# Seven block products for eight in two row pairs of the first feed-forward weight product

## The chip, the cores and the metric

One core of one Trainium2 chip. The metric is the device time of one execution of the whole program in microseconds (us), the median of several runs.

## The reference, cut to what matters

Two transformer blocks over 256 tokens of width 2048, in float32. The change is in the first block's feed-forward part:

```
h   = rmsnorm(x, ffn_norm_g)                  # 256 x 2048
hid = h @ w_ffn_in                            # 2048 x 11264, the product that changes
x   = x + (silu(hid[:, :5632]) * hid[:, 5632:]) @ w_ffn_out
```

The other large products of the first block are `h @ w_in` before it and, after it, a gate; the second block has `h @ w_up` and `@ w_down` of the same sizes.

## The kernel before, in words

Activations lie in SBUF as tiles of 128 features x 256 tokens and are the matmuls' stationary side; weights stream through as the moving side. Every float32 factor is split into a rounded part ("hi") and a remainder ("lo"), and a product is three matmuls: hi x hi, hi x lo, lo x hi, each 128 x 128 by 128 x 512.

**Granules.** A weight matrix is cut into chunks of 512 output columns, and each chunk into granules of 256 input rows (a "row pair", p): 128 partitions x 1024 columns, 512 KB. w_ffn_in has 22 chunks of 8 granules; a chunk holds 256 gate columns and the 256 up columns that belong to them. For each granule SP starts a DMA into one of four slots of `raw` (L827); ACT casts it to `wh` (L894); DVE takes the remainder into `wl` (L1242); PE does 12 matmuls (L1785), two row tiles by two token halves by three. `wh` and `wl` too have four slots: the cast of granule i waits until PE has done granule i - 4, and the DMA of granule i waits for the remainder of granule i - 4.

**Order.** One list, `plan`, holds for every step the things to do; each engine walks the same list in order and takes what is its own, waiting on semaphores. Step s holds the cast and remainder of granule s, the fetch of granule s + 4, whatever `later` put there, and the matmuls of granule s - 3. Chunk results are drained from step (last granule + 4) on.

**Drain of this stage.** `plan_gated` (L473): `silu` on ACT (L1084, L1085) from the chunk's two PSUM banks into `ST`, the first half of the scratch tile `tmp`; `gated` on DVE (L1526, L1529) multiplies it. After every second chunk, one step later, a `turn` on DVE (L1336, L1338) transposes the 512 columns of two chunks into `Y`; POOL writes `Y` to DRAM (L1742) and, two steps after the turn, gathers it back transposed as `Z` (L1750); eight steps after that, `split_hi` (ACT, L1053, L1054) and `split_lo` (DVE, L1497, L1499) make the tiles `act1` of the next product. Chunks 0 and 1 are done side by side (six granules of each, then two of each); the others one after another, in two alternating pairs of PSUM banks.

**Units of seven.** Two products of the kernel, `out1` (act1 @ w_ffn_out) and `down`, already do some row pairs another way. `product_side_by_side` (L312) runs two chunks together, a granule of one and then of the other, and at row pairs listed in `SEVEN` treats the two granules as one 2 x 2 x 2 block product done with seven block products (21 matmuls) in place of eight (24). Such a unit needs: `base_hi` (ACT, L911), a 1536-wide cast into a buffer of its own; `sums` (DVE, L1269, L1272, L1274: 1024, 512 and 512 wide) into `tile_sums`, which is `tmp`; `base_lo` (DVE, L1255), 1536 wide; `forms_hi` (ACT, L917) and `forms_lo` (DVE, L1278), 2048 wide, into two slots of `wh` and `wl`. They stand in the list in this order, in the step of the unit's second granule. PE does `multiply_base` (9 matmuls, after `base_lo`) and `multiply_forms` (12, after `forms_lo`). The fetches that reuse the two raw slots wait for `base_lo`. Four block products of each unit add up in four PSUM banks that the pair of chunks shares; after the pair's last unit `shared_out` (ACT, L930) copies them to `tile_sums`, and DVE adds them up and onto the rows `X`. The activations' own sums and differences are made once per stage (`xs_sum`, `xs_hi`, `xs_lo`).

Of the kernel before, what the change touches and what calls it, by code (L numbers as in the profile page):

```python
# [8 lines left out]
P = 128  # L9
# [35 lines left out]
SEVEN = (8, 10, 12, 14, 16, 18)  # L45
# [50 lines left out]
def two_block_kernel(nc, t, out):  # L96
    with ExitStack() as ctx:
# [124 lines left out]
        base_lo = view("base_lo", [P, 3, 512], o_a + 6 * K, FR)  # L222
        tile_sums = tmp.rearrange("p (k c) -> p k c", k=4)
        xs_hi = view("xs_hi", [P, 6, 3, P], o_a + 12 * K, FR)
        xs_lo = view("xs_lo", [P, 6, 3, P], o_a + 21 * K, FR)
        xs_in = view("xs_in", [P, 2, 4, P], o_a)
        xs_out = view("xs_out", [P, 2, 4, P], o_a + 4 * K)
# [41 lines left out]
        seven_operand = {"out1": "act1", "down": "act2"}  # L269
        side_by_side = {"out1": [], "down": []}  # L270
# [41 lines left out]
        def product_side_by_side(src, stage, q, bank, order, tail, afters, late, cleared):  # L312

            operand = seven_operand[stage]
            pair = Pair(stage, q, [], 4 - bank)
            side_by_side[stage].append(pair)
# [4 lines left out]
            rows = list(order[:tail])  # L321
            for u, p in enumerate(rows):
                if p in SEVEN:
                    former = list(seven.values())[-1] if seven else None
                    unit = Seven(len(granules), p, pair, former, SEVEN.index(p))
# [4 lines left out]
            for k, name in enumerate(("shared_out", "shared_sums", "shared_first", "shared_last", "shared_second")):  # L330
# [137 lines left out]
        def plan_x_sums(stage, step, every):  # L468
            for j in range(3):
                for k, name in enumerate(("xs_sum", "xs_hi", "xs_lo")):  # L470
                    later(step + every * j + k, lambda name=name, j=j: do(name, stage, j))

        def plan_gated(n):  # L473
            def after(s, chunk):
                chunk.drained = [("silu", n), ("gated", n)]
                do("silu", n)
                do("gated", n)

                def leave():
                    rows_of["act1", n // 2] = turn(s + 1, ST, ("gated", n))  # L480
                if n % 2:
                    later(s + 1, leave)
                    plan_split(("act1", n // 2), s + 11, "act1", n // 2)
# [95 lines left out]
        for n in range(2, 22):  # L579
            last_ffn = product(t["w_ffn_in"], "N", "ffn", PAIRS16, ("gated", n), plan_gated(n), n)  # L580
        plan_x_sums("out1", len(granules) + 4, 3)
        out_from = len(granules)
        for q in range(2):
            cleared = ([], []) if q == 0 else ([("shared_out", "out1", 0)], [("shared_out", "out1", 0)])
            product_side_by_side(t["w_ffn_out"], "out1", q, (4, 0)[q], OUT_ORDERS[q], OUT_TAILS[q],
                                 [plan_out(2 * q), plan_out(2 * q + 1)], 0, cleared)
# [74 lines left out]
        for q in range(2):  # L661
            cleared = ([("pool_out", 1)], [("x_split", 1, 1)]) if q == 0 else ([("shared_out", "down", 0)],) * 2
            product_side_by_side(t["w_down"], "down", q, (4, 0)[q], DOWN_ORDERS[q], DOWN_TAILS[q],
                                 [plan_down(2 * q), plan_down(2 * q + 1)], (5, 0)[q], cleared)
# [70 lines left out]

        def product_of(*key):
            return through(named[key])
# [51 lines left out]
        def seven_tiles(x, j):  # L789

            k = 2 * SEVEN[2 * j]
# [81 lines left out]
        def scalar(e):  # L873
# [8 lines left out]
            for name, args in phases:  # L882
# [19 lines left out]
                elif name == "base_hi":  # L902
# [4 lines left out]
                    if unit.pair.q == 0 and unit is unit.pair.units[0]:  # L907
                        e.wait_ge(*at("xs_lo", unit.pair.stage, 2))
                    else:
                        e.wait_ge(multiplied, multiply_count["multiply_base", unit.former.i])  # L910
                    e.copy(base_hi.rearrange("p k c -> p (k c)"), two_slots(raw, i)[:, 512:2048]).then_inc(done[name], 1)  # L911
# [6 lines left out]
                elif name == "xs_hi":  # L918
                    stage, j = args
                    e.wait_ge(*at("xs_sum", stage, j))  # L920
                    e.copy(seven_tiles(operands[seven_operand[stage]][0], j)[:, :, 1], xs_out[:, :, 0])
                    e.copy(xs_hi[:, 2 * j:2 * j + 2], xs_out[:, :, 1:4]).then_inc(done[name], 1)
                elif name == "shared_out":
# [5 lines left out]
                    for k in range(4):  # L929
                        e.copy(tile_sums[:, k, :], ps[:, pair.shared + k, :]).then_inc(done[name], 1)  # L930
# [145 lines left out]
                elif name == "silu":  # L1076
# [6 lines left out]
                    e.wait_ge(*product_of("gated", n))  # L1083
# [129 lines left out]
        def vector(e):  # L1213
# [22 lines left out]
            for name, args in phases:  # L1236
# [15 lines left out]
                elif name == "base_lo":  # L1252
                    i, = args
                    e.wait_ge(*at("base_hi", i))
                    e.tensor_tensor(base_lo.rearrange("p k c -> p (k c)"), two_slots(raw, i)[:, 512:2048],  # L1255
                                    base_hi.rearrange("p k c -> p (k c)").bitcast(F32), ALU.subtract).then_inc(done[name], 1)
                elif name == "sums":
# [22 lines left out]
                elif name == "xs_sum":  # L1280
                    stage, j = args
                    hi, lo = (seven_tiles(x, j) for x in operands[seven_operand[stage]])
                    if j == 0:

                        e.wait_ge(*through(last_ffn if stage == "out1" else last_up))
                    else:
                        e.wait_ge(*at("xs_lo", stage, j - 1))
                    e.wait_ge(*tile_at(seven_operand[stage], 2 * SEVEN[2 * j + 1] + 1))
                    e.tensor_tensor(xs_in[:], hi.bitcast(F32), lo.bitcast(F32), ALU.add).then_inc(vector_step, 1)  # L1289
                    e.wait_ge(vector_step, next(step))  # L1290
                    e.tensor_tensor(xs_out[:, :, 0:2], xs_in[:, :, 1:2].broadcast_to([P, 2, 2, P]), xs_in[:, :, 0:4:3],  # L1291
                                    ALU.subtract).then_inc(vector_step, 1)
                    e.wait_ge(vector_step, next(step))
                    e.tensor_tensor(xs_out[:, :, 2], xs_in[:, :, 0], xs_out[:, :, 1], ALU.subtract).then_inc(vector_step, 1)
                    e.wait_ge(vector_step, next(step))
                    e.tensor_tensor(xs_out[:, :, 3], xs_in[:, :, 2], xs_out[:, :, 2], ALU.subtract).then_inc(done[name], 1)
                elif name == "xs_lo":
                    stage, j = args
                    e.wait_ge(*at("xs_hi", stage, j))
                    hi, lo = (seven_tiles(x, j)[:, :, 1] for x in operands[seven_operand[stage]])  # L1300
# [3 lines left out]
                elif name == "shared_sums":  # L1304

                    stage, q = args
                    p1, p5, p6, p7 = (tile_sums[:, k, :] for k in range(4))
# [3 lines left out]
                    e.tensor_tensor(p7, p7, p6, ALU.add).then_inc(done[name], 1)  # L1311
                elif name == "shared_first":
# [4 lines left out]
                    e.tensor_tensor(X[:, 1, n0], X[:, 1, n0], tile_sums[:, 3, :], ALU.subtract).then_inc(done[name], 1)  # L1317
                elif name == "shared_last":
                    stage, q = args
                    e.wait_ge(*at("shared_first", stage, q))  # L1320
                    e.tensor_tensor(tile_sums[:, 2:4, :], tile_sums[:, 2:4, :],
                                    tile_sums[:, 1:2, :].broadcast_to([P, 2, 512]), ALU.add).then_inc(done[name], 1)
                elif name == "shared_second":
                    stage, q = args
                    n1 = slice(1024 * q + 512, 1024 * q + 1024)
                    e.wait_ge(*at("shared_last", stage, q))
                    e.tensor_tensor(X[:, :, n1], X[:, :, n1], tile_sums[:, 2:4, :], ALU.add).then_inc(done[name], 1)

# [436 lines left out]
        def tensor(e):  # L1765
# [42 lines left out]
            for name, args in phases:  # L1808
# [44 lines left out]
                elif name == "multiply_base":  # L1853
# [4 lines left out]
                    b11, b22, b21 = ([x[:, n, :] for x in (base_hi, base_lo)] for n in range(3))  # L1858
                    operand = seven_operand[pair.stage]
                    a11, a12 = ([x[:, k + n, 0:P] for x in operands[operand]] for n in range(2))  # L1860
                    s4 = [x[:, place, 2] for x in (xs_hi, xs_lo)]
                    if opens:
                        for phase in {("out1", 0): named["gated", 20].drained + named["gated", 21].drained,
                                      ("out1", 1): named["out1", 0].drained + named["out1", 1].drained,
                                      ("down", 0): named["up", 20].drained + named["up", 21].drained,
                                      ("down", 1): named["down", 0].drained + named["down", 1].drained}[pair.stage, pair.q]:
# [7 lines left out]
                elif name == "multiply_forms":  # L1874
# [5 lines left out]
                    s1, s2 = ([x[:, place, n] for x in (xs_hi, xs_lo)] for n in range(2))  # L1880
                    s3, a22 = ([x[:, k + n, P:T] for x in operands[seven_operand[pair.stage]]] for n in range(2))
# [129 lines left out]
def sevens(v):  # L2011
# [3 lines left out]
    for p in SEVEN:  # L2015
        first, second = v[:, 0, p].copy(), v[:, 1, p].copy()
        v[:, 0, p, :, 0], v[:, 0, p, :, 1] = second[:, :, 0], first[:, :, 0]
        v[:, 1, p, :, 0], v[:, 1, p, :, 1] = second[:, :, 1], first[:, :, 1]
# [73 lines left out]
```

## Time and profile before

| what | value |
|---|---|
| median of 3 runs | 2418.22 us (2418.18 to 2418.65) |
| the profiled execution | 2418.17 us, its span 2416.4 us |
| granted TensorE clock | 0.999 |
| PE busy | 2405.6 us (100%), 10666 matmuls |
| DVE busy | 1621.5 us (67%) |
| ACT busy | 1310.1 us (54%) |
| POOL busy | 189.4 us (8%) |
| DMA | 545.85 MB, mean 226 GB/s |

The page gives busy time by engine, the windows the same for a stretch, the timeline single instructions with start, length and, in brackets, how long the engine sat idle before and what released it. A matmul's length includes its way through the array, so that matmuls overlap. The longest idle times of the other engines are ACT's casts waiting for PE (883.7 us in 635 waits) and DVE's remainders waiting for the casts.

### The profile page before, as it was taken

What the parts mean: (1) busy time and instruction counts of PE and PEld (TensorE: products, weight loads), DVE (VectorE), ACT (ScalarE), POOL (GpSimd) and SP (SyncE); (2) the same over time, 40 slices, a digit from 0 to 9 for tenths busy, and PEclk for the clock granted to TensorE, in tenths of its full rate; (3) what the DMA queues carried; (4) which work ended last, traced back from release to release, by engine and by line L of the source; (5) the groups of instructions that cost most, each with busy time, mean ns of one, the idle gap of its engine ahead of it and who ended that gap; (6) DMA issues with size and microseconds to landing.
All of it is one profiled execution on the core that took longest, in us unless ns stands there. A gap on an engine that the chain in (4) does not pass through costs nothing.

```text
span 2416.4 us, 27837 instructions
## 1 busy us (share of the span) xinstructions
PE 2405.6 (100%) x10666; PEld 1993.9 (83%) x10666; DVE 1621.5 (67%) x2009; ACT 1310.1 (54%) x1608; POOL 189.4 (8%) x349
## 2 busy tenths in 40 slices
PE   9999999999999999999999999999999999999998
PEld 8888888888888888888888888888888888888887
DVE  7575555667555555569786865786567766678886
ACT  7555566445444444445455754545566666665554
POOL 0000000001000000000001110110111111110000
PEclk9999999999999999999999999999999999999999
DMA  8777665778777777676678777887788888886664
GB/s 278 224 223 226 200 192 178 221 233 253 221 211 226 215 212 225 210 217 210 198 230 272 243 237 216 254 249 234 238 245 245 241 244 240 240 248 209 215 204 160
DMA packets 155013, 545.85 MB, mean 226 GB/s; under 512 B 20096, under 2 KB 20608, under 8 KB 154624
## 3 DMA queue, kind: packets, MB, share of 16 engines
q1 hardware_dynamic: 131120, 470.91, 62.4%
q0 software_dynamic: 23184, 72.37, 11.2%
q8 instruction: 84, 1.38, 0.2%
q10 hardware_dynamic: 576, 0.79, 0.1%
q14 instruction: 49, 0.40, 0.1%
HBM read 505.72 MB, written 38.27 MB: 225 GB/s over the span
## 4 chain that ended last, share of the span: by engine, by line
PE 97%; DVE 2%; DMA 1%; ACT 0%; issue 0%; SPq 0%; DVEq 0%; ACTq 0%
PE ps L1785 96%; DVE wl L1242 0%; DMA raw<-in_w_down 0%; ACT wh L894 0%; PE ps L1924 0%; DMA XG<-in_x 0%; DVE xs_in L1289 0%; PE ps L1944 0%; DVE tmp L1666 0%; DVE xs_lo L1302 0%; DVE tmp L1269 0%; DVE tmp L1673 0%; DVE wl L1278 0%; DVE xs_out L1291 0%; ACT wh L917 0%
## 5 line engine op out<-in xcount | busy, mean ns | idle before, releaser
L1242 DVE TENSOR_TENSOR wl<-raw,wh 128x1024 fp32r<-128x1024 f32 x826 | 1007.1, 1222 | 749.5 <-ACT wh L894 748.5
L894 ACT CAST wh<-raw 128x1024 fp32r<-128x1024 f32 x826 | 863.8, 1049 | 897.1 <-PE ps L1785 883.7
L1785 PE MATMUL ps<-wh,x1g_hi 128*128 128x512 f32 x704 | 273.9, 389 | 0.0
L1785 PE MATMUL ps<-wl,x1g_hi 128*128 128x512 f32 x704 | 273.9, 389 | 0.0
L1785 PE MATMUL ps<-wh,x1g_lo 128*128 128x512 f32 x704 | 273.9, 389 | 0.0
L1785 PE MATMUL ps<-wh,x4g_hi 128*128 128x512 f32 x704 | 273.9, 389 | 0.0
L1785 PE MATMUL ps<-wl,x4g_hi 128*128 128x512 f32 x704 | 273.9, 389 | 0.0
L1785 PE MATMUL ps<-wh,x4g_lo 128*128 128x512 f32 x704 | 273.9, 389 | 0.0
L1785 PE MATMUL ps<-wh,h_hi 128*128 128x512 f32 x576 | 225.1, 393 | 0.8 <-ACT wh L899 0.8
L1785 PE MATMUL ps<-wh,h_lo 128*128 128x512 f32 x576 | 223.5, 390 | 0.0
L1785 PE MATMUL ps<-wl,h_hi 128*128 128x512 f32 x576 | 223.2, 390 | 0.0
L1785 PE MATMUL ps<-wh,act_hi 128*128 128x512 f32 x560 | 217.9, 389 | 0.0
L1785 PE MATMUL ps<-wl,act_hi 128*128 128x512 f32 x560 | 217.9, 389 | 0.0
L1785 PE MATMUL ps<-wh,act_lo 128*128 128x512 f32 x560 | 217.8, 389 | 0.0
L1750 POOL DMA_DIRECT2D Z<-rows x268 | 146.1, 552 | 363.9 <-DMA rows<-Y 351.7
L1742 POOL DMA_DIRECT2D rows<-Y x67 | 37.5, 560 | 1620.3 <-DVE Y L1338 1620.3
L1785 PEld LDWEIGHTS ps<-wl,x1g_hi 128*128 128x128 f32 x704 | 132.2, 188 | 27.6
L1785 PEld LDWEIGHTS ps<-wh,x4g_lo 128*128 128x128 f32 x704 | 132.1, 188 | 27.6
L1785 PEld LDWEIGHTS ps<-wh,x1g_hi 128*128 128x128 f32 x704 | 132.2, 188 | 27.3
L1785 PEld LDWEIGHTS ps<-wh,x1g_lo 128*128 128x128 f32 x704 | 132.2, 188 | 27.3
L1785 PEld LDWEIGHTS ps<-wh,x4g_hi 128*128 128x128 f32 x704 | 132.1, 188 | 27.4
L1785 PEld LDWEIGHTS ps<-wl,x4g_hi 128*128 128x128 f32 x704 | 132.1, 188 | 27.4
(348 smaller groups left out, 3560.6 us busy)
## 6 DMA issues: line engine op xcount, KB each, us to landing
raw<-in_w_in SPq DMA_DIRECT2D x196, 512.0 KB, 4.4
raw<-in_w_ffn_in SPq DMA_DIRECT2D x176, 512.0 KB, 3.7
raw<-in_w_up SPq DMA_DIRECT2D x176, 512.0 KB, 4.6
raw<-in_w_ffn_out SPq DMA_DIRECT2D x88, 512.0 KB, 4.3
raw<-in_w_down SPq DMA_DIRECT2D x88, 512.0 KB, 4.3
rows<-Y POOLq DMA_DIRECT2D x67, 512.0 KB, 5.6
Z<-rows POOLq DMA_DIRECT2D x268, 128.0 KB, 4.9
raw<-in_w_o SPq DMA_DIRECT2D x32, 512.0 KB, 4.7
```

What stands on the lines that cost most here:

```text
L894: e.copy(wh[:, i % RING, :], raw[:, slot, :]).then_inc(rounded, 1)
L1242: e.tensor_tensor(wl[:, r, :], raw[:, i % RAW, :], wh[:, r, :].bitcast(F32), ALU.subtract).then_inc(remainder, 1)
L1742: e.dma_start(rows_out[n % 2], Y[:]).then_inc(rows_left[n % 2], 16)
L1750: e.dma_start(ZA[32 * q:32 * q + 32], rows_out[n % 2, :, 256 * q:256 * q + 256].rearrange("(a i) e -> i a e", a=4)).then_inc(rows_back[n % ...
L1785: return e.matmul(dst, weights, x, start=start, stop=stop, skip_group_check=True)
```

## The change

In the first feed-forward product, eight pairs of chunks (2,3 to 16,17) run side by side. Of their eight row pairs, 4 and 6 are units of seven, in the order 0, 1, 4, 2, 6, 3, 5 and then row pair 7 of one chunk and of the other: so granules 4,5 and 8,9 of 16 are the units, and the chunks' last granules are 14 and 15. Chunks 0 and 1 stay as they were; 18 to 21 follow one after another as before, in other banks.

The pair alternates between PSUM banks 0 to 3 and 4 to 7, with the shared products in the other four. These are copied to `tile_sums` (`shared_out`), put together (`shared_sums`, `shared_last`), and, when a chunk is complete, added onto its banks in PSUM (`shared_bank`, DVE) ahead of its `silu`, which now waits for it. The first unit of a pair waits, in `sums`, for the turn of the pair before, since both use `tmp`; and PE's first shared product waits until the pair before is drained. The weights of rows 4 and 6 are swapped between the two chunks on the host, as for the other stages. Buffers for this stage (`gated_hi`, `gated_lo`, `gated_xs_hi` and so on) lie in the upper part of `act1`. In `out1` and `down` the shared tiles are put in other places and `shared_last` is two 512-wide operations in place of one of 1024.

```diff
-SEVEN = (8, 10, 12, 14, 16, 18)
+SEVEN = {"gated": (4, 6), "out1": (8, 10, 12, 14, 16, 18), "down": (8, 10, 12, 14, 16, 18)}
+GATED_PAIRS = range(1, 9)
+GATED_ORDER = (0, 1, 4, 2, 6, 3, 5, 7)
...
         def plan_gated(n):
             def after(s, chunk):
                 chunk.drained = [("silu", n), ("gated", n)]
+                if n // 2 in GATED_PAIRS:
+                    do("shared_bank", n)
                 do("silu", n)
                 do("gated", n)
...
-        for n in range(2, 22):
-            last_ffn = product(t["w_ffn_in"], "N", "ffn", PAIRS16, ("gated", n), plan_gated(n), n)
+        plan_x_sums("gated", len(granules), 0)
+        for q in GATED_PAIRS:
+            cleared = [] if q == 1 else [("shared_out", "gated", q - 1)]
+            product_side_by_side(t["w_ffn_in"], "gated", q, (0, 4)[q % 2], GATED_ORDER, 7, [plan_gated(2 * q), plan_gated(2 * q + 1)],
+                                 0, (cleared, cleared), ("shared_out", "shared_sums", "shared_last"))
+        for n in range(18, 22):
+            last_ffn = product(t["w_ffn_in"], "N", "ffn", PAIRS16, ("gated", n), plan_gated(n), n, (4, 6, 0, 2)[n - 18])
+            last_ffn.cleared = [("shared_out", "gated", 8)] if n < 20 else named["gated", n - 4].drained
...
+        def gated_at(n):
+
+            return at("shared_bank", n) if n // 2 in GATED_PAIRS else product_of("gated", n)
...
-                    e.wait_ge(*product_of("gated", n))
+                    e.wait_ge(*gated_at(n))
                     e.activation(ST[:, 0, sl], banks(chunk)[0][:, 0:T], ACT.Silu, scale=RT[:, 0:1]).then_inc(done[name], 1)
...
-                        e.wait_ge(*{("out1", 0): at("turn", rows_of["act1", 10]), ("out1", 1): at("shared_second", "out1", 0),
-                                    ("down", 0): at("act2_lo", 21), ("down", 1): at("squares", "out", 1)}[
-                                        unit.pair.stage, unit.pair.q])
+                        stage, q = unit.pair.stage, unit.pair.q
+                        e.wait_ge(*(at("turn", rows_of["act1", q - 1]) if stage == "gated" else {
+                            ("out1", 0): at("turn", rows_of["act1", 10]), ("out1", 1): at("shared_second", "out1", 0),
+                            ("down", 0): at("act2_lo", 21), ("down", 1): at("squares", "out", 1)}[stage, q]))
...
+                elif name == "shared_last":
+                    stage, q = args
+                    _, second, first, p5 = (tile_sums[:, k, :] for k in range(4))
+                    e.wait_ge(*at("shared_sums", stage, q))
+                    e.tensor_tensor(first, first, p5, ALU.add).then_inc(vector_step, 1)
+                    e.wait_ge(vector_step, next(step))
+                    e.tensor_tensor(p5, p5, second, ALU.add).then_inc(done[name], 1)
...
+                elif name == "shared_bank":
+                    n, = args
+                    bank0, bank1 = banks(named["gated", n])
+                    e.wait_ge(*product_of("gated", n))
+                    if n % 2 == 0:
+                        e.wait_ge(*at("shared_sums", "gated", n // 2))
+                        e.tensor_tensor(bank0, bank0, tile_sums[:, 0, :], ALU.add)
+                        e.tensor_tensor(bank1, bank1, tile_sums[:, 1, :], ALU.subtract).then_inc(done[name], 1)
+                    else:
+                        b = named["gated", n].bank
+                        e.wait_ge(*at("shared_last", "gated", n // 2))
+                        e.tensor_tensor(ps[:, b:b + 2, :], ps[:, b:b + 2, :], tile_sums[:, 2:4, :], ALU.add).then_inc(done[name], 1)
```

## Rows read from the trace of the kernel before

**Rows 1.** The page, part 1: busy time, share of the span and instructions of each engine.

```profile
PE 2405.6 (100%) x10666; PEld 1993.9 (83%) x10666; DVE 1621.5 (67%) x2009; ACT 1310.1 (54%) x1608; POOL 189.4 (8%) x349
```

**Rows 2.** The instructions on one operand of the feed-forward stage.

```profile
L1785 PE MATMUL ps<-wh,x1g_hi x704: 389/389/389, 593.0 to 1071.0; 128*128 128x512 f32 x176
```

**Rows 3.** Windows: length, busy PE, PEld, DVE, ACT, POOL, clock, DMA share, GB/s.

```profile
635.00:678.60 43.60, 43.60 (x194) 36.13 (x193) 23.65 (x25) 19.75 (x23) 2.74 (x5) 1.00 0.72 217
1200.96:1211.15 10.19, 10.19 (x46) 8.45 (x45) 8.84 (x8) 5.48 (x5) 0.00 (x0) 1.00 0.68 217
2236.00:2246.00 10.00, 8.94 (x38) 6.78 (x37) 8.94 (x8) 5.45 (x5) 0.00 (x0) 1.00 0.59 204
```

**Rows 4.** Timeline of DVE and ACT, one unit among dense ones (1201 to 1208).

```profile
1200.96 1.22 DVE L1269 TENSOR_TENSOR tmp<-raw 128x1024 f32<-128x1024 f32 x1
...
1202.94 0.69 DVE L1274 TENSOR_TENSOR tmp<-tmp,raw 128x512 f32<-128x512 f32 x1
1203.55 1.75 DVE L1255 TENSOR_TENSOR base_lo<-raw,base_hi 128x1536 fp32r<-128x1536 f32 x1
1205.68 2.29 DVE L1278 TENSOR_TENSOR wl<-tmp,wh 128x2048 fp32r<-128x2048 f32 x1 [0.39 <-ACT wh L917]
...
1203.74 1.92 ACT L917 CAST wh<-tmp 128x2048 fp32r<-128x2048 f32 x1 [1.46 <-DVE tmp L1274]
```

**Rows 5.** Timeline of ACT and DVE around one drained chunk, feed-forward stage.

```profile
723.78 1.05 ACT L894 CAST wh<-raw 128x1024 fp32r<-128x1024 f32 x1 [1.67 <-PE ps L1785]
724.73 0.47 ACT L1084 ACTIVATE tmp<-ps,small 128x256 f32<-128x256 f32 x1
725.10 0.47 ACT L1085 ACTIVATE tmp<-ps,small 128x256 f32<-128x256 f32 x1
...
724.86 1.22 DVE L1242 TENSOR_TENSOR wl<-raw,wh 128x1024 fp32r<-128x1024 f32 x1 [1.50 <-ACT wh L894]
726.00 0.48 DVE L1526 SCALAR_TENSOR_TENSOR tmp<-ps,small,tmp 128x256 f32<-128x256 f32 x1
726.40 0.47 DVE L1529 SCALAR_TENSOR_TENSOR tmp<-ps,small,tmp 128x256 f32<-128x256 f32 x1
...
728.73 0.70 DVE L1336 STREAM_TRANSPOSE Y<-tmp 128x512 f32<-128x512 f32 x1
729.36 0.67 DVE L1338 STREAM_TRANSPOSE Y<-tmp 128x512 f32<-128x512 f32 x1
```

**Rows 6.** Timeline of PE where a granule begins, same stretch.

```profile
723.52 0.39 PE L1785 MATMUL ps<-wh,x1g_hi 128*128 128x512 f32 x1
```

**Rows 7.** Timeline of DVE and PE, a unit of down whose load came late.

```profile
2236.53 1.23 DVE L1269 TENSOR_TENSOR tmp<-raw 128x1024 f32<-128x1024 f32 x1 [2.58 <-DMA raw<-in_w_down]
...
2239.13 1.75 DVE L1255 TENSOR_TENSOR base_lo<-raw,base_hi 128x1536 fp32r<-128x1536 f32 x1
2241.26 2.29 DVE L1278 TENSOR_TENSOR wl<-tmp,wh 128x2048 fp32r<-128x2048 f32 x1 [0.38 <-ACT wh L917]
...
2241.03 0.47 PE L1785 MATMUL ps<-base_hi,act_hi 128*128 128x512 f32 x1 [0.80 <-DVE base_lo L1255]
...
2243.61 0.50 PE L1785 MATMUL ps<-wh,xs_hi 128*128 128x512 f32 x1 [0.26 <-DVE wl L1278]
```

**Rows 8.** Loads issued 2240 to 2242, nothing beside them.

```profile
DMA to landing us min/median/max: 3.6/4.1/4.5
```

**Rows 9.** Loads issued 736 to 742, beside the gather.

```profile
L827 SPq DMA_DIRECT2D raw<-in_w_ffn_in x2: 328/328/328, 737.0 to 739.7; - x2
...
DMA to landing us min/median/max: 6.4/6.9/7.5
```

**Rows 10.** Timeline of POOL: the gather of the turned rows.

```profile
736.20 2.18 POOL L1750 DMA_DIRECT2D Z<-rows  x4 [5.05 <-DMA rows<-Y]
```

**Rows 11.** Groups by form: 512-wide on DVE, from PSUM and from SBUF.

```profile
L1680 DVE TENSOR_TENSOR tmp<-tmp 128x512 f32<-128x512 f32 x22 | 15.1, 684 | 0.0
...
L1509 DVE TENSOR_TENSOR X<-ps,X 128x512 f32<-128x512 f32 x12 | 8.2, 684 | 0.0
```

More of the change, by code:

```diff
@@ L268, in two_block_kernel @@
         seven = {}
-        seven_operand = {"out1": "act1", "down": "act2"}
-        side_by_side = {"out1": [], "down": []}
+        seven_operand = {"gated": "ffn", "out1": "act1", "down": "act2"}
+        side_by_side = {"gated": {}, "out1": {}, "down": {}}
+        onto_rows = ("shared_out", "shared_sums", "shared_first", "shared_last", "shared_second")
         turns = []
@@ L310, in product_pair, with product_side_by_side @@
                         then[n]()
-        def product_side_by_side(src, stage, q, bank, order, tail, afters, late, cleared):
+        def product_side_by_side(src, stage, q, bank, order, tail, afters, late, cleared, ends):
             operand = seven_operand[stage]
             pair = Pair(stage, q, [], 4 - bank)
-            side_by_side[stage].append(pair)
+            side_by_side[stage][q] = pair
             for n in range(2):
@@ L320, in product_side_by_side @@
                 pair.chunks.append(chunk)
-            rows = list(order[:tail])
-            for u, p in enumerate(rows):
-                if p in SEVEN:
+            for u, p in enumerate(order[:tail]):
+                if p in SEVEN[stage]:
                     former = list(seven.values())[-1] if seven else None
-                    unit = Seven(len(granules), p, pair, former, SEVEN.index(p))
+                    unit = Seven(len(granules), p, pair, former, SEVEN[stage].index(p))
                     pair.units.append(unit)
@@ L329, in product_side_by_side @@
                     granules.append((pair.chunks[n], src[2 * q + n, p], operand, 2 * p, u == 0, False))
-            for k, name in enumerate(("shared_out", "shared_sums", "shared_first", "shared_last", "shared_second")):
+            for k, name in enumerate(ends):
                 later(pair.units[-1].i + 5 + k, lambda name=name: do(name, stage, q))
@@ L1254, in vector @@
                     e.wait_ge(*at("base_hi", i))
-                    e.tensor_tensor(base_lo.rearrange("p k c -> p (k c)"), two_slots(raw, i)[:, 512:2048],
-                                    base_hi.rearrange("p k c -> p (k c)").bitcast(F32), ALU.subtract).then_inc(done[name], 1)
+                    hi, lo = (all_three(x) for x in bases[seven[i].pair.stage])
+                    e.tensor_tensor(lo, two_slots(raw, i)[:, 512:2048], hi.bitcast(F32), ALU.subtract).then_inc(done[name], 1)
                 elif name == "sums":
@@ L1316, in vector @@
                     e.tensor_tensor(X[:, 0, n0], X[:, 0, n0], tile_sums[:, 0, :], ALU.add)
[L1317 to L1322, printed above, removed]
+                    e.tensor_tensor(X[:, 1, n0], X[:, 1, n0], tile_sums[:, 1, :], ALU.subtract).then_inc(done[name], 1)
                 elif name == "shared_second":
@@ L1857, in tensor @@
                     opens, ends_here = unit is pair.units[0], unit is pair.units[-1]
-                    b11, b22, b21 = ([x[:, n, :] for x in (base_hi, base_lo)] for n in range(3))
+                    b11, b22, b21 = ([x[:, n, :] for x in bases[pair.stage]] for n in range(3))
                     operand = seven_operand[pair.stage]
                     a11, a12 = ([x[:, k + n, 0:P] for x in operands[operand]] for n in range(2))
-                    s4 = [x[:, place, 2] for x in (xs_hi, xs_lo)]
+                    s4 = x_forms(unit)[3]
                     if opens:
[L1863 to L1866, printed above, removed]
+                        former = {"out1": ("gated", 20), "down": ("up", 20)}[pair.stage] if pair.q == 0 else (
+                            pair.stage, 2 * pair.q - 2)
+                        for phase in named[former].drained + named[former[0], former[1] + 1].drained:
                             e.wait_ge(*at(*phase))
@@ L2008, in stream, with sevens @@
     return np.ascontiguousarray(v).reshape(n // 512, k // 256, P, 1024)
-def sevens(v):
+def sevens(v, pairs, chunks):
     n, k, _, _ = v.shape
     v = v.reshape(n // 2, 2, k, P, 2, 512).copy()
[L2015 to L2018, printed above, removed]
+    for q in chunks:
+        for p in pairs:
+            first, second = v[q, 0, p].copy(), v[q, 1, p].copy()
+            v[q, 0, p, :, 0], v[q, 0, p, :, 1] = second[:, 0], first[:, 0]
+            v[q, 1, p, :, 0], v[q, 1, p, :, 1] = second[:, 1], first[:, 1]
     return np.ascontiguousarray(v.reshape(n, k, P, 1024))
```

83 lines of the change are left out of this document (54 added, 29 removed).

## The prediction

> **What bounds the kernel now.** I read the page first: PE is busy for 2405.6 of 2416.4 us [rows 1], so time goes only if matmuls go or PE starts to wait. A busy time of 0.389 us per matmul isn't its price, since matmuls overlap; the start-to-start step is. The first and last of 704 starts of the feed-forward stage [rows 2] are 478.0 us apart over 703 groups of three matmuls: 478.0 / 2109 = 0.2267 us. A granule (12 matmuls) costs PE 2.72 us, a pair of chunks (16) 43.5 us, a unit of seven block products (21 matmuls) 4.76 us. The windows show DVE busy 23.65 and ACT 19.75 of 43.6 us in today's stage [rows 3]: a wide cover on average. The question is the order in which these two queues work at the boundary of two pairs.
>
> **The gain.** Each unit has 21 matmuls for 24. Eight pairs with two units: 48 matmuls fewer, 48 x 0.2267 = 10.9 us. Nothing else leaves PE.
>
> **What is added to DVE and ACT.** Per unit, sums, base_lo and forms_lo take from the start of the sums to the end of forms_lo 1205.68 + 2.29 - 1200.96 = 7.01 us; the first third of it, until the cast of the forms starts on ACT, 2.78, and base_lo is done after 4.34 [rows 4]. The two plain remainders that this replaces cost 2 x 1.14 (start to next start) [rows 5]. Per pair also come four ACT copies and four 512-wide sums of the shared products, and the bank adds. DVE is then at some 38 of 42 us. shared_out, shared_sums, shared_last and split_lo come at granules 13 to 15, where the next chunks ask nothing of DVE, and where DVE has nearly half of its time free today [rows 3]; they cost nothing. Were that cover gone, the chain from point T below would start later by as much as DVE is late there. The one-off sums of the activations (1024 + 512 + 256 + 256 columns on DVE, a cast, a 1024-wide remainder: about 5 us at such prices) fall in pair 1's first granule, beside a ring of three filled granules, 8.2 us. POOL and SP get no new DMA; the loads behind a unit wait for base_lo instead of a remainder.
>
> **The boundary, step by step.** Name the granules of a pair 0 to 15 and those of the next 0' to 15'. The first chunk ends with 14, the second with 15. Now both are drained together, at the steps of 2' and 3', and the unit 4',5' follows at once; on DVE its sums stand behind the turn of these very chunks. Let B be the first matmul of granule 15. The cast of 2', which waits for 14, starts 0.26 us later: 723.52 against 723.78 [rows 5, 6]; call that T. PE then has 15, 0', 1', 2', 3' and wants the unit at B + 13.60 and its forms (nine matmuls on) at B + 15.64.
> - Cast 2' on ACT T to T + 1.05; remainder 2' on DVE from T + 1.08, next start T + 2.22 [rows 5].
> - shared_bank of the even chunk: two 512-wide adds, 0.60 apart (as 1202.94 and 1203.55 [rows 4]), done T + 3.50 with 0.68 for the second.
> - silu starts 0.11 after the add (DVE to ACT: 1202.94 + 0.69 to 1203.74 [rows 4]), T + 3.61, second half 0.37 later, done T + 4.45; today it follows its cast at once, 723.78 to 724.73 [rows 5]. **This wait holds ACT's queue**: the cast of 3', which could start at T + 2.72, stands behind it and starts at T + 4.35, done T + 5.40.
> - gated even fits in between. Remainder 3' T + 5.43, next start T + 6.57. shared_bank odd, 1024 wide, 1.22: T + 7.79. silu T + 7.90 to 8.74. gated odd starts T + 8.40, second half T + 8.80 to 9.27. Turn: two transposes, 0.63 and 0.67 [rows 5]: T + 9.30 to 10.60. Sums start at T + 10.63.
> - base_lo done T + 14.97 = B + 15.23. From such an end to the first matmul it takes 0.15 us (2239.13 + 1.75 to 2241.03 [rows 7]): B + 15.38 against 13.60, a wait of 1.8 us. forms_lo done T + 17.64, and 0.06 on (2241.26 + 2.29 to 2243.61 [rows 7]) the forms start at B + 17.96 instead of 15.64. **The first unit costs 2.32 us of waiting.**
> - The second unit, 8',9': its two loads go out after base_lo, at T + 15.0 and 15.4. A load takes 3.6 to 4.5 us where nothing is beside it [rows 8] and 6.4 to 7.5 beside the gather of the turned rows [rows 9]; the gather is issued some 6 us after the turn (729.36 + 0.67 to 736.20 [rows 5, 10]), here at T + 16.8, right upon them. DVE is free at T + 19.8. I take 6.0, between the two, since these loads start before the gather: landed T + 21.4, forms_lo 7.01 later, forms ready at B + 28.73. PE wants them at 17.96 + 2.72 + 5.44 + 2.04 = B + 28.16. Another 0.57; none at 4.5, and with 7.5 us 2.1.
>
> Seven boundaries (pairs 2 to 8) x 2.89 = 20.2 us. Pair 1 stands behind an old-style pair without shared_bank: its sums start some 5.7 us after the cast of 3', its forms are ready 0.1 late, its loads cost 0.5: 0.6 us. After pair 8 no unit follows, and the ring of four covers the late cast: nothing. out1 and down change by one 512-wide DVE op more per pair of chunks, beside plain tail granules: nothing. The drains that the shared banks wait for end at T + 9.3, before base_lo: nothing. **Sum: -10.9 + 20.2 + 0.6 = +9.9 us**, on the profiled execution's 2418.17 (the median of the runs, 2418.22, is the same): 2428.
>
> An operation with its output in PSUM on DVE has no row here. A read from PSUM costs nothing extra: L1509 684 ns, L1680 684 ns [rows 11]. I take the bank adds at these prices. From below nothing less is likely, as they are the fastest 512-wide rows; from above, 1.37 for the wide add if it ran as two: 0.15 per boundary, 1.1 us in all. The Trainium skill (VectorE: DVE Perf Modes, The TRN2 errata) says that a DVE operation pays 120 cycles of fixed cost from PSUM and 58 from SBUF, at 0.96 GHz some 0.065 us more, against the 684 and 684 ns above [rows 11]. By that rule three adds on the chain would add an estimated 0.19 us per boundary, 1.4 us in all.
>
> **Rivals.**
> 1. *The boundary wait is shorter than summed, and gain and loss cancel (same).* The 10.9 us are used up at 1.55 us per boundary. For it: unit 2's share of 0.57 hangs on one landing, and if the cast of 3' didn't stand behind the even silu, the chain would be 1.34 us shorter: 0.98 + about 0.55 per boundary, some 2418 in all. Against: both queues work in order, and every link above has a row. Chance 0.11.
> 2. *The cover holds (faster).* The sums of 4',5' start by T + 8.3, so that forms_lo ends under granule 3' and the base products, and the loads are back in time: then all 10.9 us stay, 2407. For it: today's DVE and ACT are idle for nearly half of the stage [rows 3], and the dense units at 1200 us run without any PE wait at DVE 8.84 of 10.19 us [rows 3]. Against: those have two plain remainders between units, not two drains and a turn; and where sums came late, at 2236.53 after a load, PE did wait, 0.80 us before the base products and 0.26 before the forms [rows 7]. It decides at 0.86 us per boundary. Chance 0.07.
> 3. *The loads cost more (slower still).* Both loads of the second unit take 7.5 us: 2.1 instead of 0.57 per pair, 8 x 1.5 = 12 more, 2440. For it, [rows 9]; against, these loads start before the gather and half of each should be done. Chance 0.12.
> 4. A wait of 2 us could cost clock besides. In the window with PE's wait of 0.80 the granted clock stays at 1.00 [rows 3]; I give it no time of its own.
>
> The forecast itself has 0.70. **Range:** the first unit's wait alone (7 x 2.32 - 10.9 + 0.1) gives 2423.7, with full load cost 2440; the cancelling case reaches down to 2418. I take 2419 to 2438, which leaves out rival 2, half of rival 1 and the top of rival 3. A measurement tells 0.2%, 4.8 us, from no change: faster 0.08, same 0.12, slower 0.80.
>
> **What would show it.** PE: 48 matmuls fewer; before the base products of the first unit of pairs 2 to 8 a gap of 1.8 us, released by base_lo, and some 0.5 more before their forms. ACT: 14 silus waiting for the bank adds, the next cast 1.6 us late. DVE: sums some 10.6 us after the cast of 2'. SP: loads held by base_lo. A pair at about 45.0 us instead of 43.5. It is wrong if PE idles less than 1 us at a boundary, if the bank adds take over 0.9 us for 512 columns, or if the second unit's base_hi doesn't wait for its load.

## The result, and the profile after

| | before | after |
|---|---|---|
| time, median of 4 runs each on the same chip | 2418.41 us (2418.18 to 2418.65) | 2443.14 us (2440.53 to 2444.89) |
| ratio, 95% interval | | 1.0101 (1.0088 to 1.0113) |
| profiled execution | 2418.17 us | 2444.39 us |
| its span | 2416.4 us | 2442.6 us |

The change costs 24.7 us where 9.9 were forecast, and the time lies above the range. The page, part 1 (busy time, share of the span, instructions of each engine), to be read against [rows 1]:

```profile
PE 2405.7 (98%) x10618; PEld 1983.8 (81%) x10618; DVE 1727.2 (71%) x2122; ACT 1341.4 (55%) x1641; POOL 189.4 (8%) x349
```

PE has its 48 matmuls fewer (10618 for 10666) but is no longer always busy: its share falls from 100% to 98%. The windows say where (length; busy PE, PEld, DVE, ACT, POOL; clock; DMA share; GB/s), first the whole stage and then one pair of chunks:

```profile
593.50:1096.90 503.40, 477.86 (x2064) 386.02 (x2063) 368.78 (x393) 248.91 (x286) 30.14 (x55) 1.00 0.67 208
651.16:697.68 46.52, 43.51 (x189) 34.73 (x188) 36.40 (x38) 23.11 (x26) 2.74 (x5) 1.00 0.65 205
```

The stage has grown from 478.6 to 503.4 us, by 24.8, and PE idles in 3.0 of a pair's 46.5 us, with DVE at 36.4. The 48 matmuls should have taken 10.9 away, so PE lost 35.7 us in this stage. (The profiled execution is 26.2 us longer in all; the other 1.4 lie outside the stage. 0.6 of them is one start of PE at 1638.5 that comes late by so much, and not in the traces of e1, e5 and e8.)

**The boundary of two pairs.** Timelines of ACT and then DVE (start, duration, engine, line, operation; in brackets the idle time before it and what ended it). They answer to [rows 5]; T, the cast of 2', is at 724.51:

```profile
724.51 1.05 ACT L926 CAST wh<-raw 128x1024 fp32r<-128x1024 f32 x1 [1.67 <-PE ps L1842]
728.14 0.48 ACT L1120 ACTIVATE tmp<-ps,small 128x256 f32<-128x256 f32 x1 [2.58 <-DVE ps L1380]
...
728.87 1.05 ACT L926 CAST wh<-raw 128x1024 fp32r<-128x1024 f32 x1
732.41 0.47 ACT L1120 ACTIVATE tmp<-ps,small 128x256 f32<-128x256 f32 x1 [2.50 <-DVE ps L1384]
```

```profile
726.73 0.69 DVE L1379 TENSOR_TENSOR ps<-ps,tmp 128x512 f32<-128x512 f32 x1
727.33 0.69 DVE L1380 TENSOR_TENSOR ps<-ps,tmp 128x512 f32<-128x512 f32 x1
...
731.09 1.23 DVE L1384 TENSOR_TENSOR ps<-ps,tmp 128x1024 f32<-128x1024 f32 x1
...
735.17 1.23 DVE L1306 TENSOR_TENSOR tmp<-raw 128x1024 f32<-128x1024 f32 x1
...
737.76 1.75 DVE L1292 TENSOR_TENSOR gated_lo<-raw,gated_hi 128x1536 fp32r<-128x1536 f32 x1
```

The first silu waits 2.58 us for the bank add, and the next cast stands behind it until T + 4.36. The sums of the unit 4',5' (L1306) start at T + 10.66, base_lo (L1292) ends at T + 15.00. What PE does with that, first for the unit 4',5' and then for 8',9' (timeline of PE):

```profile
739.66 0.47 PE L1842 MATMUL ps<-gated_hi,x1g_hi 128*128 128x512 f32 x1 [1.65 <-DVE gated_lo L1292]
...
742.23 0.50 PE L1842 MATMUL ps<-wh,gated_xs_hi 128*128 128x512 f32 x1 [0.25 <-DVE wl L1315]
...
751.77 0.47 PE L1842 MATMUL ps<-gated_hi,x1g_hi 128*128 128x512 f32 x1 [1.04 <-DVE gated_lo L1292]
...
754.35 0.50 PE L1842 MATMUL ps<-wh,gated_xs_hi 128*128 128x512 f32 x1 [0.25 <-DVE wl L1315]
```

Measured from the start of the matmul before, the one at 739.66 comes 1.80 us later than the usual step of 0.23 (1.65 of it idle), the one at 742.23 comes 0.42 later. The second unit is late too: 1.20 and 0.42. Its loads (the timeline of POOL, then the loads issued 738 to 742 with the least, median and longest time until they landed):

```profile
735.69 0.56 POOL L1799 DMA_DIRECT2D rows<-Y  x1 [40.47 <-DVE Y L1395]
739.19 2.18 POOL L1807 DMA_DIRECT2D Z<-rows  x4 [2.94 <-DMA rows<-Y]
```

```profile
L859 SPq DMA_DIRECT2D raw<-in_w_ffn_in x2: 327/380/432, 739.5 to 739.9; - x2
...
DMA to landing us min/median/max: 4.5/5.9/7.2
```

The later of the two loads took 7.2 us, and the gather (L1807) was issued at T + 14.7, a third of a microsecond ahead of the loads; in [rows 10] it came 5.6 us after the write of the rows, here 3.5. Over the stage the waits add up so (engine, line, what it waited for: us in total, times, longest):

```profile
ACT gated_hi L944 <- DMA raw<-in_w_ffn_in: 45.6, 8, 7.8
...
DVE tmp L1306 <- DMA raw<-in_w_ffn_in: 24.5, 8, 5.2
PE ps L1842 <- DVE gated_lo L1292: 21.7, 15, 3.4
...
ACT tmp L1120 <- DVE ps L1380: 20.7, 8, 2.6
```

PE waited 15 times for gated_lo: seven first units and eight second ones. Taking each late start against the step of 0.2267 us, with the matmul right behind each late one, which comes 0.08 or 0.11 us later than the step once more, the first units of pairs 2 to 8 lost 7 x 2.41 = 16.9 us, and the second units of pairs 1 to 8 lost 1.6, 1.4, 1.8, 1.8, 1.8, 2.4, 5.8 and 1.6, together 18.2. With 16.9 this is 35.1 of the 35.7.

### The profile page after: what moved, and what is told of

Read it like the earlier page. It is cut to its first block, busy times and chain, and to the rows that moved or that the text cites. A ratio compares the mean times of both kernels' runs of the same rounds, so it can differ in the third digit from the quotient of the medians.

```text
span 2442.6 us, 27959 instructions
## 1 busy us (share of the span) xinstructions
PE 2405.7 (98%) x10618; PEld 1983.8 (81%) x10618; DVE 1727.2 (71%) x2122; ACT 1341.4 (55%) x1641; POOL 189.4 (8%) x349
## 3 DMA queue, kind: packets, MB, share of 16 engines
q0 software_dynamic: 23184, 72.37, 10.9%
## 4 chain that ended last, share of the span: by engine, by line
PE 85%; DVE 7%; DMA 4%; ACT 2%; issue 2%; SPq 0%; POOL 0%; ACTq 0%; DVEq 0%; POOLq 0%
PE ps L1842 84%; DMA raw<-in_w_ffn_in 2%; DVE wl L1278 1%; DVE tmp L1306 1%; ACT wh L926 1%; DVE wl L1315 1%; ACT wh L950 1%; DVE gated_lo L1292 1%; DVE tmp L1309 1%; DVE tmp L1311 1%; DMA raw<-in_w_down 0%; DVE ps L1384 0%; DMA Z<-rows 0%; DVE Y L1395 0%; DMA rows<-Y 0%
## 5 line engine op out<-in xcount | busy, mean ns | idle before, releaser
L1278 DVE TENSOR_TENSOR wl<-raw,wh 128x1024 fp32r<-128x1024 f32 x794 | 964.5, 1222 | 630.7 <-ACT wh L926 629.3
L926 ACT CAST wh<-raw 128x1024 fp32r<-128x1024 f32 x794 | 828.2, 1049 | 767.1 <-PE ps L1842 751.6
L1842 PE MATMUL ps<-wh,x1g_hi 128*128 128x512 f32 x592 | 230.3, 389 | 0.0
L1842 PE MATMUL ps<-wl,x1g_hi 128*128 128x512 f32 x592 | 230.3, 389 | 0.0
L1842 PE MATMUL ps<-wh,x1g_lo 128*128 128x512 f32 x592 | 230.3, 389 | 0.0
L1807 POOL DMA_DIRECT2D Z<-rows x268 | 146.1, 552 | 354.1 <-DMA rows<-Y 341.6
L1842 PEld LDWEIGHTS ps<-wh,x1g_hi 128*128 128x128 f32 x592 | 111.1, 188 | 23.3
L1842 PEld LDWEIGHTS ps<-wl,x1g_hi 128*128 128x128 f32 x592 | 111.1, 188 | 23.1
L1842 PEld LDWEIGHTS ps<-wh,x1g_lo 128*128 128x128 f32 x592 | 111.1, 188 | 23.0
```

Source lines behind the costliest of these rows:

```text
L926: e.copy(wh[:, i % RING, :], raw[:, slot, :]).then_inc(rounded, 1)
L1278: e.tensor_tensor(wl[:, r, :], raw[:, i % RAW, :], wh[:, r, :].bitcast(F32), ALU.subtract).then_inc(remainder, 1)
L1807: e.dma_start(ZA[32 * q:32 * q + 32], rows_out[n % 2, :, 256 * q:256 * q + 256].rearrange("(a i) e -> i a e", a=4)).then_inc(rows_back[n % ...
L1842: return e.matmul(dst, weights, x, start=start, stop=stop, skip_group_check=True)
```

## The experiments

Four questions were open. Does the chain of in-order queues make the first unit late, and do its own loads, colliding with the gather, make the second unit late (my theory, which the expectations call A)? Or is all of it one lateness, which starts at the first unit and is handed on? Or has DVE too much work in this stage (36.4 of 46.5 us), so that any order gives such a time? And do PE's waits cost more than their length, by the clock? Eight kernels ran, each an edit of the changed kernel. The third column is the sum of PE's late starts in the stage of its trace, the fourth that sum less 10.9 us, the last the measured difference of the medians.

| kernel | us, median (lowest to highest, runs) | PE late, us | less 10.9 | measured |
|---|---|---|---|---|
| the change | 2443.14 (2440.53 to 2444.89, 4) | 35.1 | +24.2 | +24.7 |
| e1_gather | 2425.43 (2424.78 to 2425.93, 7) | 17.1 | +6.2 | +7.0 |
| e2_silus | 2432.26 (2431.65 to 2432.96, 4) | 23.8 | +12.9 | +13.8 |
| e3_order | 2417.45 (2417.00 to 2418.39, 10) | 9.6 | -1.3 | -1.0 |
| e4_both | 2414.51 (2413.76 to 2415.91, 10) | 6.5 | -4.4 | -3.9 |
| e5_order_silus | 2407.68 (2407.56 to 2408.30, 4) | 0 | -10.9 | -10.7 |
| e6_all | 2407.60 (2406.90 to 2409.62, 4) | 0 | -10.9 | -10.8 |
| e7_order_gather | 2416.16 (2415.27 to 2416.90, 10) | 8.4 | -2.5 | -2.3 |
| e8_longer | 2433.96 (2433.03 to 2435.03, 4) | 25.5 | +14.6 | +15.5 |

The kernel before took 2418.43 us beside e1 to e4 and 2418.42 beside e5 to e8. In every row the late starts of the trace explain the time within 1 us, so hardly anything but PE's lateness in this stage is at stake.

**e1_gather: the gather waits until the second unit's loads have landed.**

```diff
+            held = {rows_of["act1", q - 1]: side_by_side["gated"][q].units[1].i + 1 for q in GATED_PAIRS}
...
                     e.wait_ge(*left(n))
+                    if n in held:
+                        g = held[n]
+                        e.wait_ge(landed[g % RAW], 16 * (g // RAW + 1))
```

> POOL holds the gather of the turned rows until the loads of the second unit have landed; nothing else changes. Theory A (each pair loses 2.4 us before its first unit to the order of the DVE and ACT queues, and 1.4 to 5.8 us before its second because that unit's loads share the DMA engines with the gather): the loads land in 4.5 us instead of 6.8 to 9.6, the wait at the second unit goes (18 us over eight pairs down to under 3), the 2.4 us at the first unit stay; about 2428 us. Rival B (the second unit is late because its loads are issued late, behind base_lo, whatever runs beside them): landing times stay near 7 us, 2443. Rival C (DVE has too much work per pair, so a wait that is removed comes back at the next unit): the landing gets shorter and the time stays within 3 us of 2443.

Measured: 2425.43 us, ratio to before 1.0029 (1.0018 to 1.0040), 17.7 us less than the change. The loads of the same pair, the gather behind them, and PE at the first unit (this trace runs 3.4 us ahead of the one above):

```profile
L859 SPq DMA_DIRECT2D raw<-in_w_ffn_in x2: 328/380/432, 736.1 to 736.5; - x2
...
DMA to landing us min/median/max: 3.7/4.1/4.5
```

```profile
741.57 2.19 POOL L1811 DMA_DIRECT2D Z<-rows  x4 [8.76 <-DMA raw<-in_w_ffn_in]
```

```profile
736.22 0.47 PE L1846 MATMUL ps<-gated_hi,x1g_hi 128*128 128x512 f32 x1 [1.65 <-DVE gated_lo L1292]
...
738.79 0.50 PE L1846 MATMUL ps<-wh,gated_xs_hi 128*128 128x512 f32 x1 [0.25 <-DVE wl L1315]
```

The loads of this pair land in 4.5 us at most (4.4 to 4.8 in seven pairs, 5.5 in pair 7), the gather goes out 5.3 us behind PE's start on the first unit where it went out 0.5 ahead of it, and the second unit's matmuls start without any gap. The first unit's waits are what they were, 1.65 and 0.25 us idle. So some 18 us of the change's cost hang on the collision of two loads with the gather, and the lateness isn't handed on: the first unit is as late as ever and the second not at all. That rules out B, since the loads are issued behind base_lo as before, and C, since no wait came back.

**e2_silus: both silus and gated products after the odd chunk's bank add,** so that no cast stands behind a waiting silu.

```diff
                     do("shared_bank", n)
-                do("silu", n)
-                do("gated", n)
+                    if n % 2:
+                        do("silu", n - 1)
+                        do("gated", n - 1)
+                        do("silu", n)
+                        do("gated", n)
+                else:
+                    do("silu", n)
+                    do("gated", n)
```

> Both silus and both gated products of a pair stand in the list after the second chunk's bank add, so the cast of 3' on ACT no longer waits behind the first chunk's silu. Theory A, by the same bookkeeping as before: the sums of the first unit start some 9.1 us after the cast of 2' instead of 10.6, the wait at the first unit falls from 2.4 to about 0.9 us, the one at the second unit stays (loads and PE's need both move 1.5 us earlier); 7 x 1.5 = 10.5 us less, about 2432.5. Rival C (DVE work per pair is the bound): no more than 3 us less, 2440 to 2443.

Measured: 2432.26 us, ratio 1.0057 (1.0042 to 1.0072), 10.9 us less than the change. At the first unit PE loses 0.9 us in place of 2.41: 1.5 per boundary, near the 1.34 that the prediction's first rival gave for this very hold-up. 7 x 1.53 = 10.7 of the 10.9 us. C, which gave no more than 3 us less, is ruled out here too.

**e4_both: e1 and e2 together.**

> The silus together and the gather held, both edits at once. Theory A: first unit waits about 0.9 us, second none: -10.9 + 7 x 1.1 + 1 us from the kernel before, about 2416. If the two edits are independent, the sum of their two savings. Rival C: what one edit saves the other gives back, no better than the better of the two.

Measured: 2414.51 us, ratio 0.9984 (0.9975 to 0.9993). 17.7 and 10.9 add to 28.6, and this is 28.6 below the change: the two causes are independent.

**e3_order: the units one row pair later,** granules 6,7 and 10,11 instead of 4,5 and 8,9.

```diff
-GATED_ORDER = (0, 1, 4, 2, 6, 3, 5, 7)
+GATED_ORDER = (0, 1, 2, 4, 3, 6, 5, 7)
```

> The units stand as fourth and sixth row (order 0, 1, 2, 4, 3, 6, 5, 7): granules 6,7 and 10,11. Theory A: the first unit gets 5.4 us more until PE wants it, but the shared sums now come at 0' and 1', just ahead of the drain, and put some 2 us on DVE before it, and the two plain granules between stand ahead of the unit; about 1.4 us of wait at either unit, 2425 to 2430. Rival C (DVE work per pair is the bound, and the order doesn't matter): 2440 to 2445. Rival D (only the distance from the boundary counts): first unit without wait, some 2420.

Measured: 2417.45 us, ratio 0.9997 (0.9987 to 1.0006): some 10 us below what the expectation has under A. Timeline of POOL, the loads, and the timeline of PE at one boundary:

```profile
696.47 2.18 POOL L1807 DMA_DIRECT2D Z<-rows  x4 [5.39 <-DMA rows<-Y]
```

```profile
L859 SPq DMA_DIRECT2D raw<-in_w_ffn_in x2: 328/380/432, 695.4 to 695.7; - x2
...
DMA to landing us min/median/max: 3.8/4.6/5.4
```

```profile
695.47 0.47 PE L1842 MATMUL ps<-gated_hi,x1g_hi 128*128 128x512 f32 x1 [0.36 <-DVE gated_lo L1292]
...
698.06 0.50 PE L1842 MATMUL ps<-wh,gated_xs_hi 128*128 128x512 f32 x1 [0.27 <-DVE wl L1315]
```

Two things change at once. PE comes later to the first unit but the chain is longer as well, since two more casts and remainders now stand ahead of the sums; a wait of 0.36 is left of 1.65, and 1.15 us in all. And the loads are now issued 1.1 us ahead of the gather (695.4 to 696.47), where they were 0.3 behind it: the longer one lands in 5.4 us and not 7.2. Over the eight pairs the gather comes 1.0 to 2.1 us behind the first load, and the later load takes 4.8 to 6.2 us; all second units together lose 1.5 us in place of 18.2. That second effect is what my expectation left out. The time lies nearer to rival D's 2420, but D wanted a first unit without any wait, and 7 x 1.15 us are left there; e5 tests what they are.

**e7_order_gather: e3 and e1 together.**

> Order and gather held, silus as in the changed kernel. Theory A: the 1.15 us at the first unit stay, the 1.5 us in all at the second go: about 2416. Rival E (the gather takes part in the first unit's wait too): under 2414.

Measured: 2416.16 us, ratio 0.9991 (0.9981 to 1.0000), 1.3 below e3. The first unit's 7 x 1.15 = 8.1 us stay (one of the seven loses 1.52), and E, which gave under 2414, is ruled out. In this order the collision is worth 1.3 us instead of 17.7.

**e5_order_silus: e3 and e2 together.**

> The fourth-and-sixth-row order with the silus together. The order alone left 1.15 us of excess at the first unit (7 boundaries) and 1.5 us in all at the second. Theory A (the DVE chain from the drain to the first unit's forms decides): the chain gets 1.5 us shorter, so the first unit waits for nothing, some 8 us less than the order alone: about 2409 to 2410. Rival D (the distance alone had done it, and what is left at the first unit is a fixed price of a unit): 2416 to 2417.

Measured: 2407.68 us, ratio 0.9955 (0.9940 to 0.9970): the whole gain, 1 to 2 us less than A gave, since the second unit's waits went too, and far from D's 2416, and the fastest kernel of this study with e6. The page's part 1, a window of one pair, and the same granules' operand as in [rows 2]:

```profile
PE 2395.0 (100%) x10618; PEld 1984.9 (83%) x10618; DVE 1723.5 (72%) x2122; ACT 1343.7 (56%) x1641; POOL 189.4 (8%) x349
```

```profile
735.15:777.30 42.15, 42.15 (x188) 34.90 (x187) 35.81 (x38) 23.34 (x27) 2.74 (x5) 1.00 0.73 225
```

```profile
L1848 PE MATMUL ps<-wh,x1g_hi x592: 389/389/389, 593.4 to 1060.5; 128*128 128x512 f32 x198
```

PE works through while DVE is busy for 35.81 of 42.15 us (85%), more densely than in the change (36.4 of 46.5, 78%). **So DVE's work is not the bound:** the same work in another order leaves no wait at all. The stage's starts lie 467.1 us apart, from 593.4 to 1060.5, for 478.0 in [rows 2]: 10.9 us less. Timelines of ACT and POOL at one boundary:

```profile
721.48 1.06 ACT L932 CAST wh<-raw 128x1024 fp32r<-128x1024 f32 x1 [1.67 <-PE ps L1848]
724.04 0.48 ACT L1126 ACTIVATE tmp<-ps,small 128x256 f32<-128x256 f32 x1 [1.50 <-DVE ps L1386]
...
726.28 0.48 ACT L1126 ACTIVATE tmp<-ps,small 128x256 f32<-128x256 f32 x1 [1.41 <-DVE ps L1390]
...
727.01 1.99 ACT L932 CAST wh<-raw 128x1024 fp32r<-128x1024 f32 x2
```

```profile
737.91 2.18 POOL L1813 DMA_DIRECT2D Z<-rows  x4 [6.25 <-DMA rows<-Y]
```

The cast of 3' runs at 721.48, ahead of both silus, and waits for nothing but PE. The loads, issued at 735.9 and 736.3, land in 3.5 and 5.3 us, with the gather 2.0 us behind the first.

**e6_all: e1, e2 and e3 together.**

> Order, silus together and gather held. Theory A: no wait left at either unit, 48 matmuls fewer at 0.2267 us: -10.9 us plus under 1, 2407.5 to 2408.5. Rival D: as without the silus, 2416.

Measured: 2407.60 us, ratio 0.9957 (0.9940 to 0.9974), no different from e5. With loads ahead of the gather and time in hand, nothing is left to hold.

**e8_longer: e1, and the first transpose of the eight pairs' turns done twice,** so that the first unit's wait grows by a known length and nothing else is late.

```diff
+                    if turns[n].filled[0] == "gated" and turns[n].filled[1] // 2 in GATED_PAIRS:
+                        e.transpose(YQ[:, :, 0].rearrange("p q c j -> p c q j"),
+                                    src[:, 0, :].rearrange("p (c q j) -> p c q j", c=4, q=4)).then_inc(vector_step, 1)
+                        e.wait_ge(vector_step, next(step))
```

> The changed kernel with the gather held, and the first transpose of each turn of the eight pairs done twice, with a wait between: 0.73 us more on DVE between the drain and the sums of the first unit. Theory A (that chain is what PE waits for, microsecond for microsecond): 7 x 0.73 = 5.1 us more than with the gather held, about 2430.5. Rival C (DVE's whole work of a pair is what counts: 0.7 more of some 42): between no change and 1 us more, 2425.5. Rival F (there is some slack left in the chain): under 3 us more.

Measured: 2433.96 us, ratio 1.0063 (1.0048 to 1.0078), 8.5 above e1. C (1 us at most) and F (under 3) are ruled out, and A's 5.1 is too low. The start behind the wait moves from 1.80 to 2.55 us late, 0.75 for 0.73 added; seven times that are 5.2. The other 3.3 us lie where the clock is down. Windows of 3.4 us from the end of four of the seven waits on:

```profile
692.00:695.40 3.40, 3.01 (x12) 2.25 (x13) 3.07 (x2) 2.20 (x3) 0.00 (x0) 1.00 0.70 235
737.40:740.80 3.40, 3.32 (x11) 2.54 (x12) 3.09 (x2) 2.17 (x3) 0.00 (x0) 0.72 0.66 219
...
874.70:878.10 3.40, 3.38 (x9) 2.65 (x10) 3.16 (x2) 2.10 (x3) 0.00 (x0) 0.60 0.70 227
...
966.60:970.00 3.40, 3.35 (x10) 2.65 (x11) 3.12 (x2) 2.14 (x3) 0.00 (x0) 0.64 0.72 229
```

The clock (third number from the end) is 1.00 behind four waits and 0.72, 0.60 and 0.64 behind three: there PE ran for part of the window at its lower level of 1.2 GHz. So the clock does have a small part: a start 2.55 us late may cost about 1 us more than that, one 1.80 late never did, in e1 or in the change. It isn't what made the change slow.

## Why the prediction was wrong

**Right: the direction, the chain of queues and the first unit.** The links of the chain, forecast and measured from T: even bank add ended 3.50 and 3.51; silu 3.61 and 3.63; cast of 3' 4.35 and 4.36; sums 10.63 and 10.66; base_lo ended 14.97 and 15.00. The wait before the base products was put at 1.78 us and is 1.80. The delay before the forms was put at 0.54 and is 0.42, but the matmuls right behind the two late starts come 0.08 and 0.11 us late once more, so the unit loses 2.41 us and not 2.32: seven boundaries 16.9, forecast 16.2. The gain, 48 matmuls at 0.2267 us, is confirmed by e5, whose time falls by 10.7. What I had put at nothing in this stage (the drains beside granules 13 to 15, the turn of pair 8) cost nothing: every late start of the change's stage lies in one of the fifteen units. `out1` and `down` cost nothing that shows either: e5, which has them too, gains 10.7 of 10.9 us. DVE's work, put at some 38 us a pair, is 36.4.

**Wrong: one term, the second unit's loads.** The step was "I take 6.0, between the two, since these loads start before the gather". *The gather does not come after the loads.* I carried over the 5.6 us from the write of the rows to the gather [rows 10]. But that write had shared the DMA engines with SP's loads. Here SP is held by base_lo in just that stretch, so the write goes alone. Windows between write and gather, before and after, each with its DMA queues (q1 carries SP's loads, q0 POOL's write):

```profile
730.60:736.20 5.60, 5.60 (x26) 4.65 (x25) 2.61 (x3) 2.10 (x2) 0.55 (x2) 1.00 0.83 282
...
q1 hardware_dynamic: 289, 1.05, 54.3%
q0 software_dynamic: 144, 0.52, 28.8%
```

```profile
735.70:739.20 3.50, 2.32 (x11) 1.58 (x9) 3.43 (x4) 1.25 (x1) 0.56 (x2) 1.00 0.37 150
...
q0 software_dynamic: 144, 0.52, 37.2%
```

DMA share 0.83 before, 0.37 after, no packet of a load beside the write, and 5.6 us become 3.5 (3.46 to 3.51 in all eight pairs). In e3, where SP isn't held in that stretch, they are 5.9 to 7.0. The very wait that I had written down as delaying the loads made the gather early: issued at T + 14.7 for a forecast T + 16.8, ahead of the loads. *With the gather ahead, the later load lands in 6.8 to 7.5 us, once in 9.6.* The 6.0 itself wasn't low for the order that I assumed: in e3 and e5, where the gather does follow the loads, the later one takes 4.6 to 6.2 us. So what failed is the order, and with it the price. With 7.2 us at this boundary instead of 6.0 the second unit costs 1.8 instead of 0.57; all eight 18.2 us, where the sum had 7 x 0.57 + 0.5 = 4.5. That is 13.7 us of the 14.8 that were missing. I had priced it as the third rival (7.5 us, 2440, chance 0.12) and argued it down with "these loads start before the gather and half of each should be done", of which the first half was untrue. The row that it was nearest to was [rows 9], loads beside the gather, and the queue held by base_lo was the reason to take it.

**Pair 7:** its second unit alone is 5.8 of the 18.2 us. The load took 9.6 us, PE waited 3.4 us, and the clock fell. Timeline and windows of PE:

```profile
940.92 0.47 PE L1842 MATMUL ps<-gated_hi,x1g_hi 128*128 128x512 f32 x1 [3.43 <-DVE gated_lo L1292]
...
942.42 0.63 PE L1842 MATMUL ps<-gated_hi,x1g_hi 128*128 128x512 f32 x1
942.85 0.63 PE L1842 MATMUL ps<-gated_lo,x1g_hi 128*128 128x512 f32 x1
```

```profile
937.10:942.30 5.20, 1.77 (x8) 1.19 (x7) 4.76 (x5) 3.84 (x4) 0.00 (x0) 1.00 0.11 20
942.30:945.80 3.50, 3.50 (x11) 2.59 (x10) 3.41 (x3) 0.71 (x1) 0.00 (x0) 0.51 0.85 291
```

From 942.4 the matmuls start 0.43 us apart, at a clock of 0.51, until 945.8: about 1.6 us more. So that one unit lost 5.8 us. The prediction gave the clock no time of its own; that was right for seven of eight pairs. Of the 14.8 us that were missing, the second units' 13.7 and the first units' 0.7 leave 0.4 without a place.

**The PSUM price.** Nothing was to be seen of an operation in PSUM on DVE before; now 512 columns added in place take 0.69 us and 1024 take 1.23 (L1379, L1380 and L1384 above), the prices of the same widths from SBUF. The Trainium skill (VectorE: DVE Perf Modes, The TRN2 errata) gives 62 cycles more of fixed cost from PSUM than from SBUF, an estimated 0.065 us per operation and 1.4 us in all. They don't appear in these rows; the lower bound, which the sum took, was right.

**The rivals.** The first (gain and loss cancel) needed a chain 1.34 us shorter; e2 is that kernel and shows 1.5 us at the first unit, but the second unit's loads kept it at 2432. The second (the cover holds) is what e5 makes true.

## What to carry to other kernels

Two queues that work in order are read at the one place where several drains meet, not by their average load: here the order alone, one row pair later and the waiting operations behind those that need not wait, was worth 35 us with the same work on every engine. Where an edit holds a DMA queue back, work out what else then moves *earlier* on the DMA engines, and price the held transfers by the row of the transfers that they will meet. Where a landing time depends on which of two transfers goes first, work out both their starts anew before choosing between two rows.

## What was not expected of the hardware

- Where loads and gather meet, a shift of little over 1 us between them decides. The later of two loads landed in 4.4 to 4.8 us with no gather beside it (e1, one pair 5.5), in 4.6 to 6.2 with the gather 0.9 to 2.8 behind the first load (e3 and e5), and in 6.8 to 7.6 with the gather 0.3 to 0.4 ahead (the change and e2; pair 7 took 9.6 and 9.0). Within the middle group the gap makes no clear difference, and nothing ran between 0.3 ahead and 0.9 behind. In e3 and e5 the order of the units changed too, so only e1 isolates the gather.
- Pair 7's long load isn't the gather's doing alone. With the gather held, the same pair's load is still the slowest of its kernel: 5.5 us in e1, 5.7 in e4, 5.5 in e8, where the others take 4.2 to 4.9. In the traces of these three, of the change and of e2, one packet (0.02 MB) of an instruction queue (q8) passes while pair 7's loads are in flight, and none of q8 does beside another pair's. That it is the cause isn't shown: in e6 and e7 such a packet passed beside loads that took 4.3 to 5.0 us.
- The granted clock fell to the level of 1.2 GHz after PE had waited 3.4 us in the change, after three of seven waits of 2.4 us idle (2.55 late) in e8, and after one of 2.81 in e2, shown below by windows; it stayed at 2.4 GHz after every wait of 1.65. Why four waits of e8 out of seven did nothing, though alike in the trace, isn't settled.

```profile
927.60:930.80 3.20, 0.43 (x2) 0.00 (x1) 3.05 (x3) 1.84 (x2) 0.00 (x0) 0.92 0.02 5
930.80:932.00 1.20, 1.16 (x3) 1.00 (x4) 0.93 (x1) 1.20 (x3) 0.00 (x0) 0.50 0.34 41
```

- A matmul that starts late is followed by one that comes 0.08 us (base products) or 0.11 us (forms) later than the usual step; the next ones keep the step again. A unit with two late starts loses 0.19 us beyond them.
